# Moving the 48 modulation-weight loads of the first projection from ScalarE's DMA queue to SyncE's

## The reference, cut to what matters

```python
xn = rms_norm(x, norm_g[i])
proj = jnp.einsum('bsd,de->bse', xn, w_in[i])            # 1024 x 1024 by 1024 x 4096
qa, ka, va, za, qb, kb, vb, zb = jnp.split(proj, cuts, axis=-1)   # 512 columns each
...
c_act = jax.nn.silu(c)
for l in range(DEPTH_2):
    mod = c_act @ w_mod[l] + b_mod[l]                    # 1 x 1024 by 1024 x 6144
    sh1, sc1, gt1, sh2, sc2, gt2 = jnp.split(mod, 6, axis=-1)
```

## Time and profile before

| what | value |
|---|---|
| time, median of 3 runs (lowest to highest) | 4873.33 us (4869.78 to 4875.01) |
| the profiled execution: time, span | 4873.33 us, 4871.2 us |
| busy in the span | PE 4120.9 (85%), DVE 2673.7 (55%), ACT 1490.3 (31%), POOL 1620.7 (33%) |
| the 48 loads of `WM` issued by ACT | first 129.5 us, last 417.2 us |
| mean granted clock of PE | 0.948 of full speed |
| DMA engines' busy share, 200 to 300 and 300 to 400 us | 0.65 and 0.74 |

### The profile page before, as it was taken

How to read it: one execution, slowest core, us unless ns; L and a number is a source line. 1 busy time by engine, 2 the same in 40 slices (tenths; PEclk the granted TensorE clock), 3 DMA queues, 4 the chain that set the end, 5 groups by cost and what they waited for, 6 DMA issues and landing times.

```text
span 4871.2 us, 61640 instructions
## 1 busy us (share of the span) xinstructions
PE 4120.9 (85%) x22152; PEld 3470.4 (71%) x22152; DVE 2673.7 (55%) x4781; ACT 1490.3 (31%) x2417; POOL 1620.7 (33%) x1076
## 2 busy tenths in 40 slices
PE   2999575888687898996898999688898996999998
PEld 1888465777566788885677777566787885777776
DVE  2443685522455565543767766555565543656655
ACT  2221343422232773432111111232773432121121
POOL 2432124522453560013233333443560013333331
PEclk9999888999899999997999999799999998999999
DMA  6664424611244322211222321234322221111111
GB/s 151 201 176 139 104 72 88 132 70 52 83 109 132 86 53 66 61 74 48 87 87 74 87 78 31 78 106 126 96 57 66 51 85 43 44 52 44 44 44 47
DMA packets 300711, 404.71 MB, mean 83 GB/s; under 512 B 45908, under 2 KB 224980, under 8 KB 299860
## 3 DMA queue, kind: packets, MB, share of 16 engines
q1 hardware_dynamic: 293496, 375.60, 27.8%
q10 hardware_dynamic: 6912, 25.17, 1.9%
HBM read 316.23 MB, written 93.63 MB: 84 GB/s over the span
## 4 chain that ended last, share of the span: by engine, by line
PE 60%; DVE 14%; issue 8%; DVEq 5%; POOL 4%; ACT 3%; DMA 3%; SPq 2%; POOLq 1%; ACTq 0%
PE ps L795 9%; PE ps L412 6%; DVE X L1773 6%; PE ps L414 6%; PE ps L413 6%; PE ps L785 5%; PE ps L1735 5%; PE ps L1737 5%; PE ps L1736 5%; DVEq L1772 3%; PE ps L1751 2%; PE ps L1753 2%; PE ps L1752 2%; PE ps L831 1%; POOL rs L690 1%
## 5 line engine op out<-in xcount | busy, mean ns | idle before, releaser
L369 POOL TENSOR_TENSOR WL<-RAW,WH 128x1024 fp32r<-128x1024 f32 x226 | 594.4, 2648 | 1406.4 <-ACT WH L365 1405.7
L412 PE MATMUL ps<-WH,XTh 128*128 128x512 f32 (+1 forms) x1536 | 611.6, 398 | 48.3 <-POOL XTl L461 25.1
L413 PE MATMUL ps<-WH,XTl 128*128 128x512 f32 (+1 forms) x1536 | 600.6, 391 | 0.0
L414 PE MATMUL ps<-WL,XTh 128*128 128x512 f32 (+1 forms) x1536 | 600.3, 391 | 0.0
L1773 DVE TENSOR_TENSOR X<-MY,X 128x512 f32<-128x512 f32 x512 | 514.9, 1006 | 48.8 <-issue 1.8
L365 ACT ACTIVATE WH<-RAW 128x1024 fp32r<-128x1024 f32 x226 | 230.4, 1059 | 923.0 <-PE ps L1753 594.5
L1751 PE MATMUL ps<-WH,Hh 128*128 128x512 f32 x1024 | 413.2, 404 | 89.1 <-DVE MY L1771 89.0
L1735 PE MATMUL ps<-XTh,WH 128*128 128x512 f32 x1024 | 401.4, 392 | 17.5 <-POOL XTl L461 17.5
L1753 PE MATMUL ps<-WL,Hh 128*128 128x512 f32 x1024 | 400.9, 392 | 0.0
L1752 PE MATMUL ps<-WH,Hl 128*128 128x512 f32 x1024 | 400.7, 391 | 0.0
L1736 PE MATMUL ps<-XTl,WH 128*128 128x512 f32 x1024 | 400.3, 391 | 0.0
(11 more groups left out here) (196 smaller groups left out, 7722.5 us busy)
## 6 DMA issues: line engine op xcount, KB each, us to landing
RAW<-w_all SPq DMA_DIRECT2D x232, 512.0 KB, 4.3
WM<-w_mod ACTq DMA_DIRECT2D x48, 512.0 KB, 4.3
WM<-w_mod SPq DMA_DIRECT2D x48, 512.0 KB, 3.8
QS<-QA_d SPq DMA_DIRECT2D x24, 512.0 KB, 4.3
KHs<-KA_d SPq DMA_DIRECT2D x48, 256.0 KB, 6.2
KLs<-KA_d SPq DMA_DIRECT2D x48, 256.0 KB, 7.2
VS<-VA_d SPq DMA_DIRECT2D x20, 512.0 KB, 7.3
X<-x SPq DMA_DIRECT2D x2, 4096.0 KB, 13.9
```

The lines of the kernel that those rows point to most:

```text
L369: e.tensor_tensor(w_low(n), w_raw(n), w_high(n).bitcast(F32), ALU.subtract).then_inc(w_ready, 1)
L412: e.matmul(bank, a, w, start=(kc == 0), stop=False)
L413: e.matmul(bank, b, w, start=False, stop=False)
L414: j = e.matmul(bank, a, l, start=False, stop=(kc == K - 1))
```

## The change

`Mod.load` of the first projection leaves ScalarE's program and goes into SyncE's. The index is n-2 in place of n-3, so a load is placed one step earlier, behind the weight loads of the step and ahead of all of its stores. The waits inside `Mod.load`, the slots and the adds stay as they are.

```diff
@@ proj_act
             for n in range(pj.nt + 3):
-                if pj.mod and 0 <= n - 3 < N_MOD:
-                    pj.mod.load(e, n - 3)
                 for piece in pj.plan.splits(n):
                     w_split_high(e, piece)
@@ proj_sp
             for n in range(pj.nt + 3):
                 for piece in pj.plan.loads(n):
                     w_load(e, piece)
+                if pj.mod and 0 <= n - 2 < N_MOD:
+                    pj.mod.load(e, n - 2)
                 if pj.mod and n - MOD_LAG - 12 in (2 * KC, 5 * KC):
                     pj.mod.store_gate(e, (n - MOD_LAG - 12) // KC)
```

## The result

The changed kernel takes 4898.93 us (median of 6 runs, 4896.16 to 4903.40) against 4873.42 us before (6 runs): 1.0054 times as long, 95% interval 1.0042 to 1.0067. It is 25.5 us slower. The forecast was 4881 with a range up to 4893.

A forecast was written before the change was run, and what follows sets the result against it. TensorE was taken to bound the first projection, idle 1.76 us in 270. Third-fold wait 7.2 plus clock 1.0 minus ACT's gain 0.5 gave +7.7 us on 4873.33: forecast 4881 us, range 4870 to 4893, its own range 4875 to 4888.

The forecast's parts named there:

- The loads start at the same moment: WM loads in the first projection: moved to SP, each still waits for the same add; cost 0.
- ACT's freed waits: ACT in the first projection: 48 issues and their waits removed, worth 0 to 1.8 us, 0.5 taken.
- The loop: V and Z tiles 18 to 31: write, add, load issue, store landing, next write; 6.73 and 6.81 us against 5.5 a tile.
- L: Landing time of a V or Z store behind a WM load on SP's queue; taken as 4.0 us, between 2.0 and 6.0.
- the walk: VectorE followed tile by tile from step 17's add, ended at 225.49, to tile 28's add, ending at 302.4.
- Paid at the third fold: TensorE at the third fold, ready at 295.17, waits 7.2 us for VectorE's add and does not get this back.
- within the slack of three banks: Three more Z tiles after the third fold: VectorE's lag there was taken as covered by the accumulator banks.
- Q/K tiles catching up: Q/K tiles after the Z tiles: VectorE writes no VB there and was expected to catch up.
- Clock: TensorE's clock may drop after the idle stretch at the third fold; bounds 0 and 3 us, 1.0 taken.
- The rival "worse": Stores meet weight loads too, L is 5.0 on the whole: 4890.5 us, or 4901.5 at 6.0; chance 0.06 for worse than 15.
- The rival "the store hides": Store landings stay at or under 3.4 us, the 7.2 vanish: 4873 us, give or take 2; chance 0.20.
- The rule beside it: Skill rule: the issuing engine only changes the sequencer's issue time, so the move costs only the issues of 0.33 us.

The follow-up runs named there:

- e2: Kernel before, loads of WM still issued by ACT, but SP waits for the same add as in the changed kernel: 4895.33 us, ratio 1.0048.
- e1: Changed kernel with the V or Z store of tile n-1 ahead of the WM load in SP's step: 4872.87 us, ratio 0.9999.
- e3: Changed kernel with load index n-3 in place of n-2 in SP's step: 4871.16 us, ratio 1.0000.
- e4: Changed kernel with three VB slots in place of two in the first projection: 4870.77 us, ratio 0.9996.
- e6: Changed kernel with each WM load from the fourth on cut to 512 columns (256 KB), modulation incomplete: 4884.78 us, ratio 1.0016.
- e9: Changed kernel with ACT's square of the tile ahead of its splits in steps 32 and 33: 4894.75 us, ratio 1.0041.
- e8: Changed kernel with 42 additional matmuls that nothing reads, in TensorE's idle time ahead of the third fold: 4900.78 us, ratio 1.0053.

## Why the prediction was wrong, point by point

- *The loads start at the same moment, and ACT's freed waits win nothing.* Right: in e2 the waits on the two engines end 0.06 us apart, and e1, e3 and e4 have all loads on SP and stay within 0.1% of before.
- *The loop.* Right in mechanism and place: 14 waits of VectorE in the V and Z tiles 18 to 31, taken away by a different order (e1), by one index (e3) and by a third slot (e4), which leave 7 to 10 us of these waits. The reason given for L was too narrow: e2 shows that the queue does not matter.
- *L = 4.0, and where the walk starts.* **This is the larger part of the miss.** L was too small by 0.6: the pair lands in 4.3 and 4.6, Z loops of 7.38 in place of 6.81. At the third fold the add ended at 311.29, against 302.4 in the walk, so VectorE was 8.9 us later than forecast. I had two nearby rows, 4.2 and (worked out) 3.9, and took the middle. The walk also took single operations at their undisturbed length and the start too early: tile 18 was written at 232.90, not 230.5, as the add of step 17 ended at 227.85, not 225.49 (0.86 of this was there before the loop, and VectorE waited 1.54 for ACT's high part); one landing took 5.6 (the store of 250.85).
- *Paid at the third fold, with the rest "within the slack of three banks", and Q/K tiles catching up.* **This step of the mechanism failed.** I walked to tile 28 and stopped there. The banks did not cover the lag (TensorE waited 1.9 us for them), and the loop runs on to tile 31. Behind it the transposes of tile 32 ask for VectorE's work, where the kernel before had 319.35 - (316.15 + 0.69) = 2.5 us of slack, against 7.2 at the fold. e6 shows it by itself: its fold and banks wait for nothing, its transposes 5.8 us. The prediction's own walk, carried on with its own numbers (two loops of 6.81 and one 0.53 shorter), gives the write of tile 31 at 320.1, against 305.57 in the trace of before: a lag of 14.5 us, less 2.5 of slack: 12, not 7.2. Neither error alone would have left the range: 12.0 in place of 7.2 gives 4885.8, and the measured add priced at the fold, 311.29 - 295.17 = 16.1, gives 4889.9.
- *So the 23.3 us of the stage* are those 12.0, then 330.57 - 320.1 = 10.5 us for the longer landings and the late start, and 0.8 that VectorE lost against the kernel before, where it should have caught up, from there to the normalization. That it did not catch up is the late weight load in the chain: SP comes to it only at 334.01, ACT's program has the split ahead of the square, and in e9 the same way is 4 us shorter. Only part of this can be won, as TensorE's own way ends 2.5 us earlier.
- *Clock.* It was 0.50 in 305 to 320 us, so the lower level did come, and TensorE's work there took 4 to 5 us more (an estimate: 8.6 us busy from 310 to 320 us at half the clock). But in e8, where it was mostly kept, TensorE only waited longer at the transposes. I added 1.0 us for it; as long as VectorE's way ends later, it is 0.
- *The rival "worse"* put L = 5.0 at 4890.5. It too was priced at the fold, and too low for that reason. Its upper bound, L = 6.0 at 4901.5, is nearest to the measured time by luck: no store of the loop took more than 5.6.
- *The rival "the store hides"* did not come true: the stores took 4.6 us, not 3.4 or less. The rule beside it, that only the issue time changes, fits the landings of e2 but not the time of the kernel, since the wait moved as well.

Between the stage's 23.3 us and the 25.5 of the medians lie 2.2 us that I can't assign: the profiled execution itself was only 4894.76 - 4873.33 = 21.4 us longer than that of before, within the spread of runs.

## What to carry to other kernels

A transfer that is moved into another queue takes its wait along, and everything behind it in that engine's program now waits for the same event. Ask for each of them when it is wanted, counted in steps, and how many slots cover it: here one index, one line of order or one more slot decided over 25 us, and no engine's busy share in the kernel before told of it. When a lag is followed, walk it to the end of the stretch that makes it, and then list every consumer behind it with its slack; the first one found need not be the tightest. Where two ways end within a few us, as here, shortening one of them wins little.

## What was not expected of the hardware

A 256 KB store that went out together with a load landed in 4.6 us beside 512 KB, 3.2 beside 256 KB, 2.4 beside 128 KB and 2.0 alone, and it made no difference whether the load was on its own queue 0.4 us ahead (4.3 and 4.6) or on the other queue 0.06 us ahead (4.5 and 4.6). The load pays too: 4.3 where it took 3.7 before. Where weight loads were issued close by as well, in e1 and e4 between 265 and 285 us, Z stores took 6.0 and 6.1 (medians of three and two). Why the one pair in the trace of before, a weight load with the store 0.38 us behind it, came out at 4.2 and not 4.6 stays open.
